# mLSTM merge gates: sixteen full products as eight units of seven half-size products inside the recurrence

## The reference, cut to what matters

```python
(a_q, a_f, a_i, a_z, b_q, b_k, b_v, b_o, b_ig, b_fg, b_z,
 c_r, c_k, c_v, c_wd, c_ad, c_z, g_a, g_b, g_c) = split_cols(xn @ w_in[l])
...
merged = (jax.nn.sigmoid(g_a) * (y_a @ w_br[l, 0])
          + jax.nn.sigmoid(g_b) * (y_b @ w_br[l, 1])
          + jax.nn.sigmoid(g_c) * (y_c @ w_br[l, 2]))
```

## Time and profile before

| | |
|---|---|
| three runs | 3298.12, 3301.9, 3296.45 us; median 3298.12 us |
| profiled execution | 3301.22 us, its span 3299.4 us |
| PE, DVE, ACT busy | 3255.6, 1748.0, 770.1 us (99%, 53%, 23% of the span) |
| granted clock of PE, mean | 0.994 |
| HBM read | 448.67 MB, 137 GB/s over the span |

### The profile page before, as it was taken

The page is one execution under the profiler, slowest core; times in us unless marked ns, Lnnn a source line. Parts: engine busy times, 40 slices in busy tenths (PEclk is TensorE's granted clock), DMA queues, the critical chain, the costliest instruction groups (busy, mean ns, idle before and its releaser), DMA issues.

```text
span 3299.4 us, 61922 instructions
## 1 busy us (share of the span) xinstructions
PE 3255.6 (99%) x26286; PEld 3003.9 (91%) x26286; DVE 1748.0 (53%) x3298; ACT 770.1 (23%) x2100; POOL 45.2 (1%) x83
## 2 busy tenths in 40 slices
PE   9999999999999999999999999999999999999999
PEld 7998899988999998988999997899879999988898
DVE  2545665414668651513455756666345566566652
ACT  1212322111111201211111226422131122353221
POOL 1000000000000000000000000000000000000000
PEclk9999999999999999999999999999999999999999
DMA  6453345453444304454444444433344545524432
GB/s 223 145 180 111 103 129 158 150 179 117 133 154 128 104 3 144 152 187 115 153 154 153 154 156 126 128 112 120 126 137 148 179 144 163 169 88 128 151 105 102
DMA packets 436210, 454.74 MB, mean 138 GB/s; under 512 B 25051, under 2 KB 412576, under 8 KB 435648
## 3 DMA queue, kind: packets, MB, share of 16 engines
q1 hardware_dynamic: 433344, 443.69, 42.5%
q0 software_dynamic: 2128, 5.19, 0.5%
q10 hardware_dynamic: 464, 1.90, 0.2%
HBM read 448.67 MB, written 2.10 MB: 137 GB/s over the span
## 4 chain that ended last, share of the span: by engine, by line
PE 95%; DVE 2%; ACT 1%; DVEq 1%; issue 0%; ACTq 0%; POOL 0%; POOLq 0%
PE bank L391 43%; PE bank L540 10%; PE bank L2340 9%; PE bank L319 5%; PE bank L2558 3%; PE bank L1965 3%; PE bank L1455 3%; PE bank L2450 1%; PE bank L2465 1%; PE bank L2486 1%; PE bank L2481 1%; PE bank L2475 1%; PE bank L2457 1%; PE bank L2469 1%; PE bank L2424 1%; PE bank L2544 1%
## 5 line engine op out<-in xcount | busy, mean ns | idle before, releaser
L391 PE MATMUL bank<-xnT,ring 128*128 128x128 f32 (+1 forms) x4800 | 593.0, 280 | 2.2 <-ACT wk L1115 1.0
L391 PEld LDWEIGHTS bank<-xnT,ring 128*128 128x128 f32 x4800 | 575.9, 191 | 5.7 <-issue 4.4
L540 PE MATMUL bank<-xnT,ring 128*128 128x256 f32 x1536 | 344.4, 383 | 0.4 <-ACT G L447 0.4
L391 PE MATMUL bank<-hT,ring 128*128 128x128 f32 (+1 forms) x2816 | 338.9, 279 | 0.6 <-ACT G L422 0.5
L391 PEld LDWEIGHTS bank<-hT,ring 128*128 128x128 f32 x2816 | 330.2, 191 | 1.2 <-ACT G L422 1.2
L540 PEld LDWEIGHTS bank<-xnT,ring 128*128 128x128 f32 x1536 | 290.6, 191 | 40.9 <-ACT G L447 0.6
L2340 PE MATMUL bank<-xnT,ring 128*128 128x272 f32 (+1 forms) x1344 | 310.9, 390 | 0.0
L2340 PEld LDWEIGHTS bank<-xnT,ring 128*128 128x128 f32 x1344 | 252.5, 190 | 44.5
L391 PE MATMUL bank<-G,ring 128*128 128x128 f32 (+1 forms) x2128 | 266.3, 278 | 0.0
L391 PEld LDWEIGHTS bank<-G,ring 128*128 128x128 f32 x2128 | 255.0, 191 | 0.2
L459 DVE TENSOR_TENSOR ring<-ring 128x1024 f32<-128x1024 f32 x100 | 122.5, 1225 | 236.6 <-PE bank L391 193.5
(11 more groups left out here) (632 smaller groups left out, 4304.8 us busy)
## 6 DMA issues: line engine op xcount, KB each, us to landing
ring<-in_w_in SPq DMA_DIRECT2D x155, 2048.0 KB, 8.3
ring<-in_w_out SPq DMA_DIRECT2D x16, 3072.0 KB, 11.8
ring<-in_w_out SPq DMA_DIRECT2D x16, 2048.0 KB, 10.6
ring<-in_w_br SPq DMA_DIRECT2D x12, 2048.0 KB, 8.3
ring<-in_w_in SPq DMA_DIRECT2D x6, 512.0 KB, 7.8
G<-in_x POOLq DMA_DIRECT2D x2, 1024.0 KB, 9.2
wk<-in_pool_w POOLq DMA_DIRECT2D x2, 1024.0 KB, 10.6
out<-G SPq DMA_DIRECT2D x8, 256.0 KB, 2.2
```

Source lines behind the costliest of these rows:

```text
L391: mm = pe.matmul(out_, weights[:, k, :], x(k), start=(start and k == 0), stop=(k == half - 1), skip_group_check=True)
L540: mm = pe.matmul(bank[j][:, META:T], ring[:, s, k, j * P:(j + 1) * P], xnT[:, k, META:T], start=(k == 0), stop=(k == KT - 1))
```

## The change

The sixteen gate tiles of the mLSTM branch become eight units u = 0 to 7 of two tiles each. A unit is seven products of 8 matmuls with 128 columns, with four weight sums (DVE), seven copies (ACT) and three additions (DVE). Both projection banks serve one unit (`own` and `other`). The gates are written into `G[:, 2]` and `G[:, 3]`, which are free after `gate_pair`, so `first_turned` in `hT` stays and `rwkv_dve` no longer makes it. Slots 0 to 2 hold the gate weights (unit u uses slot (u + 17) % 3), slot 3 holds the sums. The fillers are counted in matmuls: 56, 28 and 84 before the heads, 28 and 28 in each head, and 14, 16 and 26 around the two sums. In the excerpts below `...` marks what is left out.

```diff
+def gate_unit_products(pe, n):
+    x12_, x22_, x21_, x11_ = first_turned
+    s1, s2, s4 = sums
+    for _ in range(n):
+        m = gu_made["pe"].go() - 1
+        u, i, k = m // GU_MM, m % GU_MM // HALF, m % HALF
+        s = (u + 17) % 3
+        a11, a12, a21_less, a22 = quarters(s)
+        if i == k == 0:
+            pe.wait_ge(w_loaded[s], 16 * uses["pe"][s].go())
+            gu_slots.append((s, uses["pe"][s].n))
+            pe.wait_ge(proj_free, tiles["pe"].go())
+            if u:
+                pe.wait_ge(S["gu_act"], 6 * u)
+        t = tiles["pe"].n
+        own, other = bank[(t - 1) % 2], bank[t % 2]
+        end = k == HALF - 1
+        if i == 0:
+            mm = pe.matmul(own[:, META:MID], a11[:, k, :], xnT[:, k, META:MID], start=(k == 0), stop=end,
+                           skip_group_check=True)
+        if i == 1:
+            if k == 0:
+                pe.wait_ge(proj_free, t + 1)
+            mm = pe.matmul(other[:, META:MID], a12[:, k, :], xnT[:, HALF + k, META:MID], start=(k == 0), stop=end,
+                           skip_group_check=True)
+        if i == 2:
+            if k == 0:
+                pe.wait_ge(S["gu_act"], 6 * u + 1)
+                pe.wait_ge(S["gu_sum"], 4 * u + 2)
+            mm = pe.matmul(own[:, META:MID], s2[:, k, :], x22_[:, k, :], start=False, stop=end, skip_group_check=True)
+        if i == 3:
+            if k == 0:
+                pe.wait_ge(S["gu_act"], 6 * u + 2)
+            mm = pe.matmul(other[:, MID:T], s1[:, k, :], x12_[:, k, :], start=(k == 0), stop=end,
+                           skip_group_check=True)
+        if i == 4:
+            if k == 0:
+                pe.wait_ge(S["gu_act"], 6 * u + 3)
+                pe.wait_ge(S["gu_sum"], 4 * u + 3)
+            mm = pe.matmul(own[:, META:MID], a21_less[:, k, :], x21_[:, k, META:MID], start=False, stop=end,
+                           skip_group_check=True)
+        if i == 5:
+            if k == 0:
+                pe.wait_ge(S["gu_act"], 6 * u + 4)
+                pe.wait_ge(S["gu_sum"], 4 * u + 4)
+            mm = pe.matmul(other[:, MID:T], s4[:, k, :], xnT[:, HALF + k, MID:T], start=False, stop=end,
+                           skip_group_check=True)
+        if i == 6:
+            if k == 0:
+                pe.wait_ge(S["gu_act"], 6 * u + 5)
+            mm = pe.matmul(own[:, META:MID], a22[:, k, :], x11_[:, k, META:MID], start=False, stop=end,
+                           skip_group_check=True)
+        if end and i < 6:
+            mm.then_inc(S["gu_full"], 1)
+        if end and i == 6:
+            mm.then_inc(proj_full, 1)
...
+def gate_unit_copy(act, u, i):
+    t = tiles["act"].now()
+    own, other = bank[t % 2], bank[(t + 1) % 2]
+    pair = gate_pair_of(1, u)
+    d1, d2 = pair[:, 0, :], pair[:, 1, :]
+    row1, row2, row3 = gu_rows[u % 2]
+    if i < 6:
+        act.wait_ge(S["gu_full"], 6 * u + i + 1)
+    if i == 0:
+        if u == 2:
+            act.wait_ge(S["pair_done"], 1)
+        act.activation(d1[:, META:MID], own[:, META:MID], ACT.Copy).then_inc(S["gu_act"], 1)
...
+    if i == 6:
+        act.wait_ge(proj_full, tiles["act"].go())
+        act.activation(d2[:, META:MID], own[:, META:MID], ACT.Copy).then_inc(proj_free, 1)
+def gate_unit_copies(act, products):
+    while (gu_made["act"].n + 1) * HALF <= products:
+        c = gu_made["act"].go() - 1
+        gate_unit_copy(act, c // 7, c % 7)
...
+def gate_unit_sums12_dve(v, u):
+    s, used = gu_slots[u]
+    a11, a12, a21, a22 = quarters(s)
+    v.wait_ge(w_loaded[s], 16 * used)
+    if u:
+        v.wait_ge(S["gu_full"], 6 * (u - 1) + 4)
+    else:
+        v.wait_ge(S["st_full"], 4 * units["dve"].now() + 3)
+    v.tensor_tensor(sums[0], a21, a22, ALU.add).then_inc(S["gu_sum"], 1)
+    v.drain()
+    v.tensor_tensor(sums[1], sums[0], a11, ALU.subtract).then_inc(S["gu_sum"], 1)
+def gate_unit_sums34_dve(v, u):
+    a11, a12, a21, a22 = quarters(gu_slots[u][0])
+    v.tensor_tensor(a21, a11, a21, ALU.subtract).then_inc(S["gu_sum"], 1)
+    v.drain()
+    if u:
+        v.wait_ge(S["gu_full"], 6 * (u - 1) + 6)
+    else:
+        v.wait_ge(work_full, corner_full[units["dve"].now()])
+    v.tensor_tensor(sums[2], a12, sums[1], ALU.subtract).then_inc(S["gu_sum"], 1)
+def gate_unit_ends_dve(v, u):
+    pair, (row1, row2, row3) = gate_pair_of(1, u), gu_rows[u % 2]
+    d1, d2 = pair[:, 0, :], pair[:, 1, :]
+    v.wait_ge(S["gu_act"], 6 * u + 6)
+    v.tensor_tensor(d1[:, META:MID], d1[:, META:MID], row1, ALU.add)
+    v.tensor_tensor(d1[:, MID:T], d1[:, MID:T], row3, ALU.add)
+    v.tensor_tensor(d2[:, MID:T], d2[:, MID:T], row2, ALU.add).then_inc(S["gu_dve"], 1)
...
 def merge_pe(pe, b):
     if b == 2:
         pe.wait_ge(S["y_ready"], 3)
+    if b == 1:
+        pe.wait_ge(S["gu_act"], 6 * 8)
...
 def merge_dve(v, b):
-    tiles["dve"].go(KT)
+    tiles["dve"].go(8 if b == 1 else KT)
+    if b == 1:
+        gate_unit_ends_dve(v, 7)
...
 def mlstm_pe(pe):
     c = ml["pe"]
     evicted = tiles["pe"].n + 2
-    gates_pe(pe, 2)
+    gates["pe"].go(KT * KT)
+    gate_unit_products(pe, 56)
     pe.wait_ge(proj_free, evicted)
     pe.wait_ge(S["st_dve"], units["pe"].n)
     to_tokens_pe(pe, g[1])
-    gates_pe(pe, 1)
+    gate_unit_products(pe, 28)
     pe.wait_ge(S["ml_pe"], c["pe"].go(2))
     u = work["pe"].go()
     pe.wait_ge(work_free, u)
...
-    gates_pe(pe, 3)
+    gate_unit_products(pe, 84)
...
-        gates_pe(pe, 1)
+        gate_unit_products(pe, 28)
...
-        gates_pe(pe, 1)
-    gate_products(pe, 8)
+        gate_unit_products(pe, 28)
+    gate_unit_products(pe, 14)
     pe.wait_ge(S["ml_pe"], c["pe"].go())
     sums_pe(pe, g[4], B_HEADS, ones, per=2)
-    gate_products(pe, 9)
+    gate_unit_products(pe, 16)
     pe.wait_ge(S["ml_act"], 1 + B_HEADS + 1)
     sums_pe(pe, g[5], B_HEADS, ones, per=2)
-    gate_products(pe, 15)
+    gate_unit_products(pe, 26)
...
-    gates_act(act, 2)
+    gates["act"].go(KT)
+    gate_unit_copies(act, 56)
     to_tokens_act(act)
-    gates_act(act, 4)
+    gate_unit_copies(act, 168)
     for h in range(B_HEADS):
+        gate_unit_copies(act, 168 + 56 * h + 8)
         act.wait_ge(S["ml_in"], c["in"].go())
...
-        gates_act(act, 2)
+        gate_unit_copies(act, 168 + 56 * (h + 1))
     act.wait_ge(S["ml_in"], c["in"].go())
     act.activation(flat(g[5]), flat(g[4]), ACT.Square).then_inc(S["ml_act"], 1)
-    gates_act(act, 1)
+    gate_unit_copies(act, 422)
     act.preload_act_table(ACT.Ln)
     act.wait_ge(S["ml_in"], c["in"].go())
     act.activation(g[0][:, 0:4], g[0][:, 0:4], ACT.Ln)
     act.drain()
     act.activation(g[0][:, 0:4], g[0][:, 0:4], ACT.Exp, scale=-0.5).then_inc(S["ml_act"], 1)
-    gates_act(act, 1)
+    gate_unit_copies(act, 448)
...
+        else:
+            gate_unit_sums12_dve(v, 0)
+            gate_unit_sums34_dve(v, 0)
         unit_ends_dve(v, dst[:, j, :], dst[:, j + 1, :])
...
+    v.drain()
+    v.nop().then_inc(S["pair_done"], 1)
+    gate_unit_sums12_dve(v, 1)
+    gate_unit_sums34_dve(v, 1)
+    gate_unit_ends_dve(v, 0)
...
+    for i in (2, 3):
+        gate_unit_sums12_dve(v, i)
+        gate_unit_sums34_dve(v, i)
+        gate_unit_ends_dve(v, i - 1)
...
-    v.nop().then_inc(S["ml_pe"], 1)
+        if h == B_HEADS - 1:
+            v.nop().then_inc(S["ml_pe"], 1)
+        gate_unit_sums12_dve(v, h + 4)
+        gate_unit_sums34_dve(v, h + 4)
+        gate_unit_ends_dve(v, h + 3)
...
-    turn_inputs_dve(v, *first_turned)
...
-    section_load(sp, w_in[0], G_COL + D, 2)
+    for u in range(8):
+        c0, i = G_COL + D + BLK * u, (u + 17) % 3
+        slot_load(sp, i, w1[:, :, c0:c0 + BLK])
+        last_use[i] = (proj_full, tiles["sp"].go())
+    last_use[3] = (S["gu_dve"], 8)
     merge_load(sp, 1)
...
-    pe.wait_ge(S["st_turned"], count["pe"]["st_turned"].go())
```

More of the change, by code:

```diff
@@ L109 @@
 NAMES = [f"w_loaded{s}" for s in range(SLOTS)] + """
-proj_full proj_free gate_out part_used work_full work_free turn_full turn_free heads_done merge_done meta_sq meta_h
+proj_full proj_free gu_full gu_act gu_sum gu_dve pair_done gate_out part_used work_full work_free turn_full turn_free heads_done merge_done meta_sq meta_h
 const_in stack_in stack_zero w_q0 w_q1 w_q2 x0_half x1_half warm_in gain_in gain_turned gain_ready row_full x0_in x1_in m_in eye_in levels_in x_sq x_rstd diag_ready x_back bias_in vectors_turned vectors_ready rms_sq rms_acc rms_rstd rows_in xn_ready raw_in seam_out h_tile out_tile out_full out_last y_tile y_ready
@@ L543, in gate_products, with gate_pair_of @@
                     mm.then_inc(proj_full, 1)
+        GU_MM = 7 * HALF
+        gu_made = {e: Turn() for e in ("pe", "act")}
+        gu_slots = []
+        gu_rows = [[sum_space[:, 3328 + 384 * i + P * j:3328 + 384 * i + P * (j + 1)] for j in range(3)] for i in range(2)]
+        def gate_pair_of(b, u):
+            if b == 1:
+                return G[:, 2 + u // 4, 2 * (u % 4):2 * (u % 4) + 2, :]
+            return hT[:, 2 * u:2 * u + 2, :]
```

(27 more changed lines are left out.)

## The result

The changed kernel takes 3307.72 us (median of 11 runs, 3303.92 to 3311.54) against 3298.89 for the kernel before (11 runs, 3296.44 to 3303.13). The ratio is 1.0025 with a 95% interval of 1.0016 to 1.0034: slower by 5 to 11 us, in the middle 8. The profiled execution has a span of 3305.9 us where the one before had 3299.4. It was 662.07 to 814.87 before, 152.8 us; it is now 661.22 to 822.61, 161.4 us. The difference of 8.6 us is as large as the 8.8 us between the medians.

What follows compares the result with a forecast made beforehand. The prediction took PE's stream as the bound, busy for 95% of the last chain. Its terms, -11.9 + 3.0 + 2.45 + 8.4 + 2.0 + 1.7 = +5.65 us on a median of 3298.1, gave 3303.8 us, range 3297 to 3309.

Steps and rivals of the forecast that it cites:

- the first rival: At the two ACT waits: both, not one, are followed by low clock; sum +7.4, 3305.5 us; chance 0.32.
- Fillers, -11.9: Gate work on PE: eight units take 100.1 us where sixteen tiles took 112.0, a gain of 11.9 us.
- First ACT wait, 3.0: Unit 7's third product waits for the copy of the first, queued behind ACT's Square: PE idle 3.0 us.
- Second, 2.45: Unit 7's sixth product waits for the copy of the fourth, behind ACT's Ln and Exp: PE idle 2.45 us.
- Load, 8.4: The first merge matmul waits for a 2 MB load into slot 0, issued only at the gates' end: 8.4 us.
- Clock behind the load, 2.0: After the idle time at the merge PE runs below full clock: 2.0 us lost, bounds 1.0 and 3.6.
- Clock behind the ACT waits, 1.7 for both together: Low PE clock behind unit 7's two waits for ACT copies: one loss of 1.7 us, bounds 0 and 3.6.
- DVE in the heads, nothing: In the heads, DVE's added sums and additions run late but leave 1.4 us of slack and cost nothing.
- the rival of late heads: DVE's sums push the scores late and PE waits in three heads: +8.7, 3306.8 us; chance 0.06.
- the hidden load: At the merge, PE's other work covers the wait for slot 0: -4.75, 3293.4 us; chance 0.07.
- nothing waits: ACT serves the gate copies early and the merge's load is hidden; the 11.9 gain stays whole: 3286.2 us; chance 0.07.
- narrow products at the price of wide ones: In the gate units, a narrow matmul costs what a wide one costs: +84, 3382 us; chance 1 in 100.

Runs made afterwards that it cites:

- the version with both edits: The changed kernel with the merge's weights in the slots that come free first and the last gate copies ahead of ACT's Square, Ln and Exp: 3289.52 us.
- the run with idle matmuls: The changed kernel with 18 idle matmuls of 272 columns between the last gate product and the first merge matmul: 3304.25 us.
- two other runs: The changed kernel with only the last gate copies moved ahead on ACT, 3299.35 us; the kernel before with only its last eight gate tiles' slots changed, 3312.65 us.
- the run with the other slots: The changed kernel with the merge's weights in slot order 1, 2, 0, 3 in place of 0, 1, 2, 3: 3296.11 us.

## Why the prediction was right, and where it was off

The direction, the three waits with their places and causes, and the range were right: 3303.8 was forecast, 3307.7 measured, inside 3297 to 3309. The likeliest case was not what came; the first rival was, with the clock lowered behind all three waits. The largest chance, 0.50, was on a change within 0.2%; the measured 0.25% lies above that, though its interval reaches down to 0.16%. Of the 3.9 us between forecast and measurement, 0.8 are the base (3298.9 for the kernel before in 11 runs, 3298.1 in the three that were shown) and 2.9 the stretch (8.6 for 5.65). The bounds were not added up as they were stated: the upper sum takes 2.2 for the clock behind the load, whose bound was given as 3.6; with 3.6 it would be 11.7 us, 3309.8, just outside the range. By its own steps:

- *Fillers, -11.9.* Without the waits the stretch shortens by 10.1 us. One whole unit takes the 12.51 us of the earlier trace rows (661.22 to 673.73), but a unit cut in two by other products loses 0.1 us at most places where PE changes over: 1.89 us for a product that starts a head (704.99 to 706.88) where others take 1.79. So one sign that the prediction named as proving it wrong, a gate unit longer than 12.6 us, did come: a head's unit takes 12.8 (6.35 from 704.99 and 6.45 from 714.90). A head's period became 18.51 us (704.99 to 723.50), not 18.3. Four heads make 0.8 of the missing 1.8; 0.3 lie at the merge's start in the version with both edits (L605 at 794.90, merge at 796.96, 2.06 us for 1.79), which the changed kernel doesn't show for its wait. Of the last 0.7, about 0.3 lie in the two units ahead of the heads, one of which is cut too (25.3 us for 25.0), and 0.4 in the old tiles: the first two took 13.81 and the last three 20.8 where 7.0 each were reckoned. Why a change of products costs 0.1 us no run shows.
- *First ACT wait, 3.0:* 2.8 by the starts. *Second, 2.45:* 2.3. *Load, 8.4:* 8.3. All three to 0.2 us, and each vanished when its named cause was taken away.
- *Clock behind the load, 2.0:* 2.0 by the run with idle matmuls, 2.5 and 2.8 in two other runs. Close, but loosely priced: the five slow pairs of rows 8 by themselves give 2.3, since the next pair took 0.46 us and not 0.5 (2416.95 to 2421.51, then 2421.96).
- *Clock behind the ACT waits, 1.7 for both together.* Beside the fillers this was the step that failed in size: the first cost 1.7 us (3.43 for 1.79, then 0.1), the second 1.8 (799.88 to 802.75 is 2.87 for 1.79; the last product ended near 805.3, 2.5 for 1.79). I had two rows of about that length, one with a loss and one without, and took one loss; both came. The same two stretches were slow again in the run with the other slots (3.66 and 3.09 us for 16 records) and in the run with idle matmuls: in all three traces that have these waits each lost 1.7 to 1.8 us. But the 2.81 us of rows 8 lost nothing, so such a wait is better priced with its clock, and whether it pays that price stays open.
- *DVE in the heads, nothing:* right; DVE's scores start 1.0 to 1.4 us after the filler where 1.1 was reckoned, PE's heads have no bracket, and the rival of late heads falls. *Input differences, nothing:* right.
- *Rivals that fell:* the hidden load (the wait is there), nothing waits (only in the version with both edits), narrow products at the price of wide ones, and with it the estimate worked out from the Trainium skill's figures (TensorE: Matmul & The Clock Gate, Back-to-back issue gap): 16 records of 128 columns take 1.79 us in the gate units too, half of what 256 columns take.

With the measured terms, and -10.4 for the fillers without those 0.3, -10.4 + 2.8 + 2.3 + 8.3 + 1.7 + 1.8 + 2.0 = +8.5 us, where the stretch shows +8.6.

## What to carry to other kernels

When filler work gets fewer buffers or a new order, look first at which buffer its last use sets free: a load that had been issued 60 us ahead of its use came to be issued at the use, and PE stood for 8 us, because its slot was freed last; four numbers in a table gave it back. When a product needs an eviction, the queue of the evicting engine becomes part of PE's order, so the evictions must stand ahead of that engine's own long waits. And when work is moved into a stream that has no idle time, sum the microseconds with the clock that each new idle time may cost, since here it was 3.5 us behind 5.1 us of the two shorter waits and 2.0 to 2.8 behind some 8 to 9 of the long one.

## What the runs showed that I had not expected

- A stream of 128-column products loses 0.1 us at most places where PE changes over between the gate's products and the recurrence's: 1.89 us for a product of 16 records at the start of a head, 1.79 elsewhere.
- The same load of 2 MB, first of four issued within some 5 us and with nothing ahead of it, let PE start 7.9, 8.2, 8.9 and 9.05 us after its issue in four kernels. No run shows why it varies by over 1 us.
- The extra DVE work in the heads reached PE through ACT's queue, one product earlier than by the direct way.
